# Down weights of the experts on ScalarE's DMA queue instead of SyncE's

## The reference

```python
def moe(x, w_router, b_router, w1, b1, w2, b2):
    logits = (xt @ w_router) + b_router                 # 32 experts
    top_val, top_idx = lax.top_k(logits, TOP_K)         # 4 for each token
    gates = jax.nn.softmax(top_val, axis=-1)
    ...                                                 # tokens sorted by expert
    hid = x_pad[toks] @ w1[e] + b1[e]                   # up: 1024 -> 2 x 1024
    glu = jnp.minimum(hid[..., :D_FF], 7.0)
    lin = jnp.clip(hid[..., D_FF:], -7.0, 7.0)
    act = glu * jax.nn.sigmoid(1.702 * glu) * (lin + 1)
    return (act @ w2[e] + b2[e]) * wts[:, None]         # down: 1024 -> 1024
```

## Time and profile before

| | |
|---|---|
| time, median of 3 runs | 1712.82 us (1712.39 to 1714.06) |
| the profiled execution | 1715.02 us, its span 1712.9 us |
| TensorE busy (matmul) | 1597.4 us, 93% |
| VectorE, ScalarE, GpSimd busy | 37%, 12%, 20% |
| SP's queue (q1) | 463.06 MB, 67.0% of 16 DMA engines' span |
| mean granted clock of TensorE | 0.975 |

### The profile page before, as it was taken

One profiled execution on the slowest core, in us unless ns is written; L12 is line 12 of the kernel. 1 busy time (PEld: TensorE's weight loads), 2 busy tenths in 40 slices (PEclk: granted clock), 3 DMA queues, 4 the chain that ended last, 5 costly groups with the idle time before them and its releaser, 6 DMA issues.

```text
span 1712.9 us, 32610 instructions
## 1 busy us (share of the span) xinstructions
PE 1597.4 (93%) x13993; PEld 802.0 (47%) x13993; DVE 633.6 (37%) x1103; ACT 200.4 (12%) x430; POOL 348.9 (20%) x400
## 2 busy tenths in 40 slices
PE   7999999999999998999989998989899898999886
PEld 5676765555458855243433333433333333433334
DVE  4665457344444535542322321311313221313125
ACT  2211112222221011010000000000000000000001
POOL 1221123000017703312121122121121211121201
PEclk9999999999999999999999999989999999999999
DMA  7442433111115363799999999999999999999996
GB/s 260 149 136 69 141 101 97 52 38 52 37 53 180 104 247 137 281 402 417 430 423 425 425 411 418 415 422 413 427 397 428 424 424 402 420 425 427 422 428 276
DMA packets 91967, 498.18 MB, mean 291 GB/s; under 512 B 9280, under 2 KB 58672, under 8 KB 74000
## 3 DMA queue, kind: packets, MB, share of 16 engines
q1 hardware_dynamic: 78304, 463.06, 67.0%
q0 software_dynamic: 13040, 32.61, 5.6%
q10 hardware_dynamic: 496, 0.56, 0.1%
HBM read 477.56 MB, written 23.89 MB: 293 GB/s over the span
## 4 chain that ended last, share of the span: by engine, by line
PE 73%; DMA 23%; issue 2%; DVE 1%; POOL 0%; SPq 0%; ACT 0%; POOLq 0%; ACTq 0%; DVEq 0%
PE PS L2225 26%; DMA ring<-in_w 20%; PE PS L514 12%; PE PS L2237 8%; PE PS L2020 7%; PE PS L2106 6%; PE PS L2131 3%; PE PS L2056 2%; PE PS L1977 2%; PE PS L2071 2%; DMA ring<-y_dram 1%; PE PS L2060 1%; PE PS L2045 1%; DMA mix_sb<-xt_dram,ints 1%; PE PS L1852 1%
## 5 line engine op out<-in xcount | busy, mean ns | idle before, releaser
L2225 PE MATMUL PS<-ring,mix_sb 128*32 128x512 f32 x5376 | 611.1, 613 | 57.7 <-DMA ring<-in_w 57.6
L2225 PEld LDWEIGHTS PS<-ring,mix_sb 128*32 128x32 f32 x5376 | 174.5, 113 | 476.4 <-issue 392.6
L2237 PE MATMUL PS<-ring,hm_sb 128*32 128x256 f32 x5376 | 296.6, 379 | 1.8 <-DMA ring<-in_w 1.8
L1734 DVE TENSOR_TENSOR low_sb<-PS,low_sb 128x1536 f32<-128x1536 f32 (+1 forms) x32 | 49.9, 1558 | 606.7 <-PE PS L2225 606.7
L2237 PEld LDWEIGHTS PS<-ring,hm_sb 128*32 128x32 f32 x5376 | 173.4, 110 | 132.5 <-issue 18.9
L929 POOL COPY ints<-ints 128x3 int32 (+1 forms) x30 | 5.6, 187 | 675.4 <-ACT hm_sb L1162 675.4
L1156 ACT ACTIVATE hm_sb<-hm_sb 128x768 f32<-128x768 f32 (+1 forms) x32 | 24.5, 765 | 706.5 <-DVE hm_sb L1736 706.5
L874 POOL DMA_INDIRECT mix_sb<-xt_dram,ints x84 | 86.6, 1031 | 64.1 <-issue 22.2
L900 POOL DMA_INDIRECT y_dram<-hm_sb,ints x80 | 80.9, 1011 | 43.3 <-POOL ints L929 25.5
L514 PE MATMUL PS<-uT_sb,ring 128*128 128x512 f32 (+2 forms) x240 | 78.2, 483 | 0.0
L1747 DVE STREAM_TRANSPOSE hm_sb<-mix_sb 128x768 f32<-128x768 f32 (+1 forms) x32 | 45.3, 1417 | 77.3 <-PE PS L2237 77.3
(11 more groups left out here) (376 smaller groups left out, 1579.5 us busy)
## 6 DMA issues: line engine op xcount, KB each, us to landing
ring<-in_w SPq DMA_DIRECT2D x58, 4096.0 KB, 20.2
ring<-in_w SPq DMA_DIRECT2D x72, 2048.0 KB, 15.9
ring<-in_w_in SPq DMA_DIRECT2D x24, 512.0 KB, 5.3
ring<-in_w_in SPq DMA_DIRECT2D x8, 1024.0 KB, 5.3
y_dram<-at_sb POOLq DMA_DIRECT2D x4, 2048.0 KB, 11.2
ring<-in_w SPq DMA_DIRECT2D x8, 1024.0 KB, 5.3
ring<-y_dram SPq DMA_DIRECT2D x4, 2048.0 KB, 25.1
x_sb<-in_x SPq DMA_DIRECT2D x8, 512.0 KB, 8.3
```

Source lines behind the costliest of these rows:

```text
L1734: V.tensor_tensor(hid, PS[:, at:at + g, :], b1_row.unsqueeze(1).broadcast_to([P, g, 2 * QR]), ALU.add).then_inc(hid_used, 1)
L2225: last = nc.tensor.matmul(PS[32 * j:32 * j + 32, at + t, :].rearrange("p (c n) -> p c n", c=2), xgT[n][:, k, 32 * t:32 * t + 32], w1_c[k][ ...
L2237: last = nc.tensor.matmul(PS[32 * j:32 * j + 32, Y_BANK + t, 0:QR], actT[:, k, 32 * t:32 * t + 32], w2_in[k // 2][:, k % 2, j * QR:(j + 1) ...
```

## The change

SP's calls of `load_down` in the expert loop are taken out; its queue keeps the up weights, the last expert's down weights and all that stood on it before and after the loop. ScalarE gets a `load_down(e)` of its own: after it has copied the output rows of expert e - 1 it reads the number of expert e and issues both pairs of its down weights on its own queue, for e from 1 to 30. It waits for nothing more than the copy already waits for (`pe_y`, the down of e - 1 done, and `y_out`, the stores from the same buffer two experts ago). The first pair is thus issued after the whole down instead of after its half. Ahead of its loop ScalarE waits once for the order of the experts.

```diff
@@ SyncE
         load_up_pairs(2, expert_of(2))
-        load_down(1, 1)
         with sp.Fori(3, E) as i:
             load_up(i, expert_of(i))
-            load_down(i - 1, expert_of(i - 1))
         last_expert = expert_of(E - 1)
@@ ScalarE
+        def load_down(e):
+
+            expert = act.value_load(ids_i[0:1, bass.ds(e, 1)], min_val=0, max_val=E - 1)
+            for c in range(2):
+                act.dma_start(w2_pair[c], w2v[:, bass.ds(expert, 1), 4 * c:4 * c + 4, :].rearrange("p e k n -> p (e k n)")).then_inc(chunk_in[8 + 2 * c], 16)
+
         def expert_act(i, r, more=True):
             e = i * PERIOD + r
             sigmoid(e, groups_at(i, r))
@@
             if not isinstance(i, int) or e > 0:
                 y_rows_at(i, r - 1)
-
+                if not isinstance(i, int) or e < E - 1:
+                    load_down(e)
+
+        act.wait_ge(pos_used, IDS_KNOWN)
         for r in range(PERIOD):
             expert_act(0, r)
```

## The result

| | before | after |
|---|---|---|
| time, median | 1713.09 us (1712.39 to 1714.06) | 1765.87 us (1765.33 to 1767.35) |
| ratio | | 1.0313, 95% interval 1.030 to 1.0326 |
| profiled span | 1712.9 us | 1763.7 us |
| granted clock, mean | 0.975 | 0.957 |

The change makes the kernel slower by 52.8 us, 3.1%. The forecast was 1756 us, slower.

The account below looks back on a forecast made before the run. The weight traffic on the DMA engines was taken as the bound. Idle engines 12, clock dips 21 and PE's loop-body starts 10 us made 43 us over the 1712.82 us median: 1756 us, range 1712 to 1776.

Parts of the forecast that it names:

- What bounds the kernel: Expert loop: weight traffic on the DMA engines sets the pace; relieving SP and ACT's added work are worth 0 us.
- Turn by packet: Engines shared by two queues: turns go by packet, so up weights (32 KB) get two thirds, down weights (16 KB) one third.
- The sum: Whole kernel: three terms, 12 + 21 + 10 = 43 us, added to the median of 1712.82 us.
- my cycle: Experts of 3, 3 and 2 groups in the loop: 95.4 us, 1.3 more than the bytes, 9.3 times.
- the holes: DMA engines idle before late-issued down loads: 1.3 us per cycle of three experts, 12 us in all.
- the stop: PE's 6.2 us at the start of its loop body: 3.45 us of engine idling, three times, 10 us.
- The clock term: PE at half clock after mid-down waits of 4.8 and 6.05 us: 2.3 us per three experts, 21 us.
- The bounds: Added time overall: 12 us without clock and loop-start terms, 62 us with every delay of PE passed on whole.
- Same: Rival for the whole kernel: engines stay full whatever the order, bytes set the time, 1710 to 1716 us; chance 0.13.
- faster: Rival for the loop: two queues keep the engines fuller, at most 30 us gained, 1683 to 1709 us; chance 0.07.
- Slower by the holes alone: Rival for the loop: clock dips fall where SP's queue has work, 1717 to 1739 us, say 1725; chance 0.22.
- Far slower: Rival for the loop: waits feed themselves, fetches and gathers queue too, over 1776 us, say 1800; chance 0.08.

Follow-up runs that it names:

- act_from2: Changed kernel with the down weights of expert 1 left on SP's queue, ScalarE issuing those from expert 2 on: 1760.3 us, 1.0266.
- act_fill2: Changed kernel with unused PE products before mid-down waits, ten at experts 7, 13, 19, 25, three at 10, 16, 22, 28: 1756.2 us, 1.0243.
- act_up16: Changed kernel with each 4 MB up half, from expert 3 on, issued as two 2 MB loads in 16 KB pieces: 1740.4 us, 1.0149.

## Why the prediction was right, point by point

**What bounds the kernel: right.** The time went with the idle time of the DMA engines, and neither the relieved SP nor ACT's added work shows anywhere. ACT's issues took 0.85 us for two. One cost that I had put at 0 is visible without effect: a gather's transpose now waits for its rows (gathers land after 13.4 us, median, up to 20.6), 103.6 us in all on DVE between 770 and 1640 us, where it was 11.9 before; PE never waited for it in the changed kernel.

**Turn by packet: right, and shown.** In the changed kernel between 1148 and 1156 us, a stretch in which both queues had loads under way nearly all the time (packets, MB, share):

```profile
q1 hardware_dynamic: 66, 2.16, 63.7%
q10 hardware_dynamic: 67, 1.02, 30.2%
```

The same number of packets, twice the bytes: two thirds and one third. Before, only the packet counts of a large and a small queue had pointed there. The transfer records of this stretch, joined end to start into sixteen rows, one for each engine, show the turn itself: of 112 pairs of large pieces that follow each other on an engine, 108 are of different queues. So the turn goes by single pieces, 1.22 us for 32 KB and 0.61 us for 16 KB (medians of 770 to 1640 us), and not by loads, each of which has 128 pieces, eight for each engine. The experiments with pieces of 8, 16 and 32 KB bear it out from the other side.

**Where the waits go: right.** Foretold were some 18 waits of 4 to 10 us in the middle of the down, those at the ups shrinking to little, and 400 GB/s; measured were 17, nine of them of 4.7 to 9.9 us and eight of only 1.6 to 3.4, 8.2 us at the ups, and 401. Down loads landed 22.7 us after their issue (median; foretold 20 to 28), those of up halves after 18.3 (foretold under 20).

**The sum: near in size, its parts were not.** It gave 43 us, measured were 52.8. The starts of PE's loop body, every six experts, cut the loop in pieces. Before (start, us, idle before), then after:

```profile
861.50 0.40 PE L2216 MATMUL PS<-b_part,b_sel 128*32 128x512 bf16 x4 [3.02 <-issue]
...
1433.52 0.62 PE L2216 MATMUL PS<-b_part,b_sel 128*32 128x512 bf16 x4 [6.11 <-issue]
...
1646.90 8.77 PE L2225 MATMUL PS<-ring,mix_sb 128*32 128x512 f32 x64 [3.98 <-DMA ring<-in_w]
```

```profile
876.77 0.40 PE L2223 MATMUL PS<-b_part,b_sel 128*32 128x512 bf16 x4 [2.58 <-issue]
...
1467.80 0.40 PE L2223 MATMUL PS<-b_part,b_sel 128*32 128x512 bf16 x4 [3.20 <-issue]
...
1695.23 13.91 PE L2232 MATMUL PS<-ring,mix_sb 128*32 128x512 f32 x128
```

The last row of each is the up of expert 31. Up to the up of expert 6 the changed kernel is 15.3 us behind, over the 18 experts of the middle it loses 19.0, over the last seven 14.0 (34.3 to 48.3), and 2.5 in the tail (50.8, the difference of the spans).

- In the middle my cycle was too dear. Per six experts it gave 2 x 1.3 for the holes, 2 x 2.3 for the clock and 3.4 for the stop, 10.6 us; three times that is 32, measured were 19.0. The waits do not repeat every three experts: in place of 4.8 and 6.05 us twice, the three loop bodies of six experts have waits inside downs of 2.64, 5.01, 2.94 and 3.24 us, of 9.93, 3.04 and 2.79, and of 9.71, 1.56 and 8.53. Windows of 5 or 6 us around the holes at the four stops of PE (DMA share 0.78, 0.69, 0.72 and 0.52) give holes of 1.1 to 2.9 us and not 3.45.
- At the start I had 4/3 cycles, some 5 us, and nothing for the first load on the new queue; measured were 15.3. The engines idled for some 5.5 us at 742 us (DMA share 0.31 from 741 to 749 us), since SP's queue had no backlog yet there, and PE waited 5.0 us; the run act_from2 prices this load alone at about 8 us.
- At the end I had 2 cycles, some 7 us, for 14.0. The last experts have two groups each, one behind the other, so an up of 13.8 us is all the time that a down's weights get; the waits there are 9.88 and 5.69 us.

So the step that failed is the one that took one cycle for all 28 experts. That the sum came within 10 us is in part luck: the middle was 13 us too dear, start, end and tail together some 20 us too cheap. **The clock term** (21 us) is supported in kind, not in size: act_fill2 took away four of the dips and gained 12 us. Its condition, a dip after waits above some 4 us, did not hold: half downs took 7.07 and 7.08 us after waits of 3.04 and 2.94 us, and 5.39 after 3.24. **The bounds** of 12 to 62 held, and the range did.

**Rivals.** Same and faster fell with the result. Slower by the holes alone (1725, at most 1739) fell with the result as well, and act_fill2 shows that dips cost time here. Far slower did not come about. The rule of the Trainium skill in "DMA: Bandwidth & Descriptors", section Issuing engines are not separate DMA queues, that loads from several engines interleave on the same sixteen, agrees with the trace. Read as "a second queue brings no bandwidth" it is right as well, 420 and 401 GB/s; read as "a second queue costs nothing" it is not.

No version beat the kernel before. The nearest with two queues is act_up16 at 1.0149.

## What to carry to other kernels

Where the DMA engines are the bound and the buffers hold just one round, as here, the order of the loads is part of the schedule: one queue that issues in the order of need is a priority, and two queues throw it away. Before moving large loads to another queue, compare the pieces per partition of the two: in these runs the turn went by packet, so the queue with the smaller pieces got the smaller share. And a wait on an engine that is not the bound costs where its end is what frees the bound's next work.

## What the runs showed of the hardware that I had not expected

- A load of 2 MB into 64 of the 128 partitions took nearly twice the DMA engines' time per byte (0.53% against 0.28% of 870 us per MB), though the sixteen engines were 95% busy, and slowed the other queue's loads too: q1 needed 49.5% for 153.95 MB, 0.32% per MB, against 0.27% in the changed kernel. A piece of 32 KB took 2.49 us (median) there and 1.22 with 128 partitions. Why was not tried.
- Halving the pieces of the up weights from 32 to 16 KB on a single queue cost 0.3% (1.0022 to 1.0042), with the same 420 GB/s in the loop.
- The second half of a down took 7.07 us after a wait of 9.93 us, 7.87 after 5.22 and 5.39 after 0.92, full clock being 5.39: PE work that computes nothing, put into the waits, made the changed kernel 12 us faster by the ratios. The length of the wait alone does not tell: in the changed kernel a half down took 7.08 us after 2.94 us and 5.39 after 3.24.
